# Modulation weights through four 1 MB buffers, and the first norm's statistics inside the prologue

## The reference

```python
m_lat = jnp.split((silu(c) @ ada_w[i] + ada_b[i])[:, None, :], 6, axis=-1)   # ada_w: (2, 1024, 6144)
m_ctx = jnp.split(silu(c_ctx) @ ada_w[i] + ada_b[i], 6, axis=-1)
h = rmsnorm(x, norm1_g[i]) * (1 + m[1]) + m[0]          # shift m[0], scale m[1]
x = x + m[2] * mixer(h)                                 # gate m[2]
x = x + m[5] * swiglu(rmsnorm(x, norm2_g[i]) * (1 + m[4]) + m[3])
filt = sin-MLP over positions (33 -> 64 -> 64 -> 2*512), times a window; then its Fourier transform
```

## Time and profile before

| | us |
|---|---|
| median of three runs | 3553.22 (3545.87 to 3558.02) |
| the profiled execution, its own time | 3556.72 |
| its span | 3555.1 |
| TensorE matmul busy | 3253.5 (92%) |
| VectorE busy | 1560.7 (44%) |
| ScalarE busy | 952.2 (27%) |
| GpSimd busy | 357.5 (10%) |
| modulation loads | 32 of 1536 KB, 7.7 from issue to landing (median) |

### The profile page before, as it was taken

How to read it: one execution, slowest core, us unless ns; L and a number is a source line. 1 busy time by engine, 2 the same in 40 slices (tenths; PEclk the granted TensorE clock), 3 DMA queues, 4 the chain that set the end, 5 groups by cost and what they waited for, 6 DMA issues and landing times. The chain is left out here.

```text
span 3555.1 us, 37659 instructions
## 1 busy us (share of the span) xinstructions
PE 3253.5 (92%) x15050; PEld 2512.4 (71%) x15050; DVE 1560.7 (44%) x1826; ACT 952.2 (27%) x1085; POOL 357.5 (10%) x252
## 2 busy tenths in 40 slices
PE   5878998799965799999999999899987899999999
PEld 2337885455554678888888888777766788888887
DVE  5305315666678533333223322567665432342333
ACT  2124112344411213111111111376773311111111
POOL 3000000077721110000000000200001000000000
PEclk8878999799987999999999999899998999999999
DMA  6772210000211411111111111201102111111112
GB/s 244 276 276 88 85 50 3 0 1 1 115 56 42 154 35 30 36 37 40 39 36 36 42 37 36 80 30 38 35 30 104 51 53 48 47 47 47 47 47 77
DMA packets 45560, 228.95 MB, mean 64 GB/s; under 512 B 6376, under 2 KB 6760, under 8 KB 39178
## 3 DMA queue, kind: packets, MB, share of 16 engines
q1 hardware_dynamic: 41594, 203.37, 16.6%
q10 hardware_dynamic: 1728, 13.63, 0.9%
q0 software_dynamic: 2128, 10.36, 0.7%
HBM read 201.65 MB, written 25.69 MB: 64 GB/s over the span
## 5 line engine op out<-in xcount | busy, mean ns | idle before, releaser
L252 PE MATMUL bank<-h_hi,w_hi 128*128 128x512 f32 (+1 forms) x2616 | 704.5, 369 | 15.3 <-DVE h_lo L1645 7.2
L252 PE MATMUL bank<-h_lo,w_hi 128*128 128x512 f32 (+1 forms) x2616 | 701.3, 368 | 0.0
L252 PE MATMUL bank<-h_hi,w_lo 128*128 128x512 f32 (+1 forms) x2616 | 700.7, 368 | 0.0
L238 DVE TENSOR_TENSOR w_lo<-w_raw,w_hi 128x1024 fp32r<-128x1024 f32 x194 | 262.6, 1354 | 662.8 <-ACT w_hi L232 658.0
L252 PEld LDWEIGHTS bank<-h_hi,w_hi 128*128 128x128 f32 x2616 | 452.9, 188 | 100.4 <-issue 15.7
L252 PEld LDWEIGHTS bank<-h_lo,w_hi 128*128 128x128 f32 x2616 | 453.0, 188 | 88.4 <-issue 3.1
L252 PEld LDWEIGHTS bank<-h_hi,w_lo 128*128 128x128 f32 x2616 | 452.7, 188 | 85.3
L1577 DVE SCALAR_TENSOR_TENSOR x<-bank,c_mods,x 128x1024 f32<-128x1024 f32 (+3 forms) x280 | 271.8, 1006 | 254.9 <-PE bank L252 254.8
L232 ACT ACTIVATE w_hi<-w_raw 128x1024 fp32r<-128x1024 f32 x194 | 203.8, 1051 | 647.2 <-PE bank L252 610.5
L252 PE MATMUL bank<-hid_hi,w_hi 128*128 128x512 f32 (+1 forms) x880 | 242.3, 373 | 11.6 <-DVE x L1577 11.6
L252 PE MATMUL bank<-hid_lo,w_hi 128*128 128x512 f32 (+1 forms) x880 | 240.1, 370 | 0.0
(11 more groups left out here) (284 smaller groups left out, 3673.3 us busy)
## 6 DMA issues: line engine op xcount, KB each, us to landing
w_raw<-in_weights SPq DMA_DIRECT2D x194, 512.0 KB, 3.5
ada_w<-in_ada_w SPq DMA_DIRECT2D x32, 1536.0 KB, 7.7
x<-in_x SPq DMA_DIRECT2D x2, 5120.0 KB, 18.6
h_gate<-u_scratch SPq DMA_DIRECT2D x4, 2560.0 KB, 9.3
u_scratch<-uc POOLq DMA_DIRECT2D x12, 640.0 KB, 3.2
spec_lat<-f_spec ACTq DMA_DIRECT2D x2, 3584.0 KB, 10.3
h_spec<-spec_lat SPq DMA_DIRECT2D x2, 3584.0 KB, 12.5
x_kept<-x SPq DMA_DIRECT2D x1, 4096.0 KB, 13.0
```

The source lines that it names most:

```text
L238: e.tensor_tensor(k.w_lo[s][:, :], k.w[s][:, :], k.w_hi[s][:, :].bitcast(F32), ALU.subtract).then_inc(k.split_lo[s], 1)
L252: mm = e.matmul(out[:, c:c + m], w[:, c1:c1 + P], x[:, c:c + m], start=(first and kk == 0 and n == 0), stop=(last and kk == kt - 1 and n = ...
```

## The change

- A modulation load holds two output tiles (`ADA_M = 2`, 1 MB), and there are 48, through four buffers. The SP issues them in an unrolled list; the one that reuses a buffer waits for the products four loads before. All loads share the semaphores for products, rows and columns.
- TensorE makes the products of load n and then turns the row of load n - 1. Products of load n wait until load n - 2 is stored. ScalarE copies row n, then stores the columns of load n - 1.
- 12 loads (`ADA_AT`) go in each product block, 1 behind each of the latent residues 2 to 6, and 14 are left for the end.
- In the order of loads the transform table goes ahead of x, and the modulation loads wait for the first hidden layer's matmuls. The clearing of `ss` waits for those of the second. `w12`, `w3` and the norm's `rr` are placed elsewhere.
- After the context transform of order 0 TensorE makes the first norm's sums and broadcasts in the prologue; the filter tiles of order 1 wait for the last copy to `rr`. VectorE scales and inverts behind its context butterfly, then makes the coefficients of norm 0 alone, which need the first eight loads. ScalarE takes root and copies to `rr` behind its store of the context spectrum.
- In `even_in` the norm begins with `xr = x * rr`. The other coefficients are made at the end of VectorE's list there (one bias addition for the first gate, one for the rest, and twelve small operations).

```diff
@@ class Norm
-        self.rr = k.at(f"rr{n}", R0 + T, [P, T])
+        self.rr = k.at(f"rr{n}", R0 + T if n else R0 + 5504, [P, T])
...
     def vector(self, k, e):
+        self.invert(k, e)
+        self.apply(k, e)
...
     def scalar(self, k, e):
+        self.root(k, e)
+        self.modulate(k, e)
@@ class Stream
-ADA_M = 3
+ADA_M = 2
 ADA_LOADS = 2 * 48 // ADA_M
+ADA_BUFS = 4
+ADA_FIRST = 2 * KT // ADA_M
...
     def load(self, k, e):
-        for s in range(2):
-            e.dma_start(self.w[s][:, :, :], k.d["ada_w"][s]).then_inc(self.full[s], 16)
-        with e.Fori(0, ADA_LOADS // 2 - 1) as i:
-            for s in range(2):
-                e.wait_ge(self.sums[s], i + 1)
-                e.dma_start(self.w[s][:, :, :], k.d["ada_w"][i * 2 + (s + 2)]).then_inc(self.full[s], 16)
+        for n in range(ADA_LOADS):
+            if n >= ADA_BUFS:
+                e.wait_ge(self.sums, n - ADA_BUFS + 1)
+            e.dma_start(self.w[n % ADA_BUFS][:, :, :], k.d["ada_w"][n]).then_inc(self.full[n % ADA_BUFS], 16)
+
+    def turn(self, k, e, n):
+        s = n % 2
+        e.wait_ge(self.read, n + 1)
+        for m in range(ADA_M):
+            tr = e.matmul(self.turned[s][:, 2 * m:2 * m + 2], self.row[s][:, m * P:(m + 1) * P],
+                          k.c["pick"][:, :], start=True, stop=True)
+        tr.then_inc(self.columns, 1)
 
     def products(self, k, e, count):
-        with e.Fori(0, count) as n:
...
+        for n in range(self.made, self.made + count):
+            s, w = n % 2, self.w[n % ADA_BUFS]
+            e.wait_ge(self.full[n % ADA_BUFS], 16 * (n // ADA_BUFS) + 16)
+            if n >= 2:
+                e.wait_ge(self.stored, n - 1)
+            for half in range(2):
+                for j in range(4):
+                    kk = 4 * half + j
+                    mm = e.matmul(self.group[s][j], k.silu_c[:, 32 * kk:32 * kk + 32], w[:, kk, :],
+                                  start=(half == 0), stop=(half == 1))
+            mm.then_inc(self.sums, 1)
+            if n:
+                self.turn(k, e, n - 1)
...
     def copy(self, k, e, count):
-        with e.Fori(0, count) as n:
...
+        for n in range(self.copied, self.copied + count):
+            s = n % 2
+            e.wait_ge(self.sums, n + 1)
+            if n >= 2:
+                e.wait_ge(self.columns, n - 1)
+            e.activation(self.row[s][:, :], self.out[s], ACT.Copy).then_inc(self.read, 1)
+            if n:
+                self.store(k, e, n - 1)
@@ prologue
+            e.dma_start(tab[:, :], d["tab_f"]).then_inc(tab_landed, 16)
             e.dma_start(k.x[:, :, :], d["x"]).then_inc(x_landed, 16)
-            e.dma_start(tab[:, :], d["tab_f"]).then_inc(tab_landed, 16)
...
+            e.wait_ge(mm_full, 1)
             ada.load(k, e)
...
+                    if g == NT:
+                        e.wait_ge(k.rr_ready, len(norm.chunks))
...
-                ada.products(k, e, 4)
+                ada.products(k, e, ADA_AT[order])
...
-                        if part == "lat" and pos in (2, 4):
+                        if part == "lat" and pos >= 2:
                             ada.products(k, e, 1)
-            ada.products(k, e, ADA_LOADS // 2 - ada.made)
+                if order == 0:
+                    e.wait_ge(hw_ready, NT)
+                    norm.tensor(k, e)
+            ada.products(k, e, ADA_LOADS - ada.made)
+            ada.turn(k, e, ADA_LOADS - 1)
...
-            ada.coefficients(k, e, steps)
+                if order == 0:
+                    norm.invert(k, e)
+                    e.wait_ge(others, 16 * len(names))
+                    e.wait_ge(ada.stored, ADA_FIRST)
+                    ada.coefficients(k, e, steps, [0])
...
                 e.dma_start(d["spec_" + part][order], spec[:, 0:2 * npos[part], :]).then_inc(stored, 16)
+                if j == 1:
+                    norm.root(k, e)
...
             e.memset(k.silu_c[:, :], 0.0).then_inc(padded, 1)
-            for s in range(2):
-                e.sem_inc(ada.stored[s], 1)
+            e.wait_ge(mm_full, 2)
             e.memset(k.ss[:, :], 0.0).then_inc(cleared, 1)
@@ even_in
-            norm.tensor(k, e)
             first_pair(k, e, w0, a0, k.rhs_h, (T, T), k.h_ready, norm.h_base)
...
-            norm.scalar(k, e)
+            norm.modulate(k, e)
...
-            norm.vector(k, e)
+            norm.apply(k, e)
...
             fold_gains(k, e)
+            k.ada.gate_bias(k, e, coef_steps)
+            k.ada.coefficients(k, e, coef_steps, [1, 2, 3])
```

More of the change, by code:

```diff
@@ L340, in scalar, with root @@
     def scalar(self, k, e):
+        self.root(k, e)
+        self.modulate(k, e)
+    def root(self, k, e):
         t, n = self.tiles, self.n
@@ L372, in __init__ @@
         words = KT * ADA_M * P
[L373 to L379, removed]
+        places = (S0, S0 + words, END - 2 * words, END - words)
+        assert 2 * words <= 4 * WS and H0 + 29056 <= END - 2 * words
+        self.w = [k.at(f"ada_w{n}", at, [P, KT, ADA_M * P]) for n, at in enumerate(places)]
+        self.full = [k.sem(f"ada_landed{n}") for n in range(ADA_BUFS)]
+        self.sums, self.read, self.stored, self.columns = (k.sem(f"ada_{n}") for n in ("sums", "read", "stored", "columns"))
         self.row = [k.at(f"ada_row{s}", H0 + 28544 + s * ADA_M * P, [P, ADA_M * P]) for s in range(2)]
@@ L386, in load @@
     def load(self, k, e):
-        for s in range(2):
-            e.dma_start(self.w[s][:, :, :], k.d["ada_w"][s]).then_inc(self.full[s], 16)
-        with e.Fori(0, ADA_LOADS // 2 - 1) as i:
-            for s in range(2):
-                e.wait_ge(self.sums[s], i + 1)
-                e.dma_start(self.w[s][:, :, :], k.d["ada_w"][i * 2 + (s + 2)]).then_inc(self.full[s], 16)
-    def products(self, k, e, count):
-        with e.Fori(0, count) as n:
-            i = n + self.made
-            for s in range(2):
[L399 to L412, removed]
@@ L413, in products, with store @@
         self.made += count
+    def store(self, k, e, n):
+        s = n % 2
+        e.wait_ge(self.columns, n + 1)
+        e.activation(k.mods[:, 2 * ADA_M * n:2 * ADA_M * (n + 1)], self.turned[s], ACT.Copy).then_inc(self.stored, 1)
     def copy(self, k, e, count):
-        with e.Fori(0, count) as n:
[L418 to L421, removed]
-            for s in range(2):
-                e.wait_ge(self.columns[s], i + 1)
-                e.activation(k.mods[:, bass.ds(i * (4 * ADA_M) + 2 * ADA_M * s, 2 * ADA_M)], self.turned[s], ACT.Copy
-                             ).then_inc(self.stored[s], 1)
+        for n in range(self.copied, self.copied + count):
+            s = n % 2
+            e.wait_ge(self.sums, n + 1)
[4 more added lines that the diff above has]
+                self.store(k, e, n - 1)
@@ L426, in copy, with coefficients @@
         self.copied += count
-    def coefficients(self, k, e, steps):
-        for s in range(2):
-            e.wait_ge(self.stored[s], ADA_LOADS // 2 + 1)
+    def coefficients(self, k, e, steps, norms):
+        first, last = 24 * norms[0], 24 * norms[-1] + (16 if len(norms) == 1 else 24)
         mods = k.mods[:, :].rearrange("p (m w) -> p m w", w=2)
-        bias = k.ada_b[:, :].unsqueeze(2).to_broadcast([P, 96, 2])
-        steps(e.tensor_tensor(mods, mods, bias, ALU.add))
-        for n in range(4):
+        part = mods[:, first:last, :]
+        bias = k.ada_b[:, first:last].unsqueeze(2).to_broadcast([P, last - first, 2])
+        steps(e.tensor_tensor(part, part, bias, ALU.add))
+        for n in norms:
@@ L442, in coefficients, with gate_bias @@
                 steps(e.tensor_copy(b, shift))
+    def gate_bias(self, k, e, steps):
+        mods = k.mods[:, :].rearrange("p (m w) -> p m w", w=2)[:, 16:24, :]
+        bias = k.ada_b[:, 16:24].unsqueeze(2).to_broadcast([P, 8, 2])
+        steps(e.tensor_tensor(mods, mods, bias, ALU.add))
 def butterfly_lat(e, steps, x, y, t):
@@ L706, in _ @@
                 if part == "lat":
-                    ada.copy(k, e, 4)
+                    ada.copy(k, e, ADA_AT[order])
                 if j:
@@ L718, in _ @@
                 e.dma_start(d["spec_" + part][order], spec[:, 0:2 * npos[part], :]).then_inc(stored, 16)
-            ada.copy(k, e, ADA_LOADS // 2 - ada.copied)
+                if j == 1:
+                    norm.root(k, e)
+            ada.copy(k, e, ADA_LOADS - ada.copied)
+            ada.store(k, e, ADA_LOADS - 1)
             e.wait_ge(stored, 64)
```

20 lines of the change are left out of this document (12 added, 8 removed).

## The result

| | before | after |
|---|---|---|
| median of five runs, us | 3553.22 (3545.87 to 3558.02) | 3572.93 (3569.28 to 3575.03) |
| profiled execution, its own time | 3556.72 | 3569.28 |
| its span | 3555.1 | 3567.6 |
| TensorE matmul busy | 3253.5 | 3275.0 |

The change makes the kernel slower by 19.7 us: the ratio of the times is 1.0053, with its 95% interval from 1.0040 to 1.0066. The forecast was 3549, and the range ended at 3567, 5.9 us short.

The account below looks back on a forecast made before the run. The prologue was taken as one chain on TensorE, whose products and DMA take turns. Its stages summed to xr at 273.8 instead of 278.1, net -4.3 us, so 3553.2 - 4.3 = 3549 us; range 3533 to 3567.

Parts of the forecast that it names:

- wait ahead of the tail: Before the last 14 loads: TensorE waits for ScalarE's store, context copies, root's table and row copy, 16.8 us.
- the one on the tiles: Filter tiles of order 1: they run at the high clock behind the norm's broadcasts, 9.6 us instead of 17.43.
- the 30 us for the second block: Second product block: twelve loads, between 26.6 us (fast) and 36.2 (slow), taken as 30.
- rival A: Tiles of order 1 and second block: low clock after TensorE's idleness, +14 us, 3563 in all; chance 0.27.
- the load beside the store: Spectrum stores: a modulation load sharing the DMA adds 0 to 2.4 us, taken as 2, and 1 at the tail.
- Rival C: Both spectrum stores share the engines with up to four loads, up to +14 us more, 3563; chance 0.05.
- The chain through ScalarE: Norm in the prologue: store, its wait, context copies, next store, table and root precede the broadcasts; 23.0 us with these.
- The hand-over: Product stream: one bare wait per load from the turn's end through the column store to the next products, 0.34 us.
- the cycle: Product stream, per 1 MB load: products, turn and hand-over, 3.15 us at 1.2 GHz, 1.77 at 2.4.
- A forward block starts slow: Forward blocks: the clock begins low and becomes fast, 1 to 4 us for the slow start.
- Rival B: Product blocks and tail: products keep 2.4 GHz and the DMA paces all, net -20 us, 3533; chance 0.15.
- Rival D: Norm's move: free, as ScalarE's wait overlaps nothing new, sum -18 us, 3535; chance 0.05.

Follow-up runs that it names:

- f1: The kernel after with twelve unused matmuls between the norm's sums and broadcasts and one more behind the broadcasts: 3559.55 us, 1.0009 of before.
- e7: The kernel after with the five woven loads behind residues 1 to 5 instead of 2 to 6: 3562.99 us, 1.0020 of before.
- e2: The kernel before with only the norm's move into the prologue, its loads and two buffers as before: 3573.27 us, 1.0045 of before.
- e1: The kernel after with the first norm put back to the start of the input projection, four buffers kept: 3551.35 us, 0.9985 of before.
- e4: The kernel after with the norm behind the context transform of order 1 and its root behind the latent store: 3545.50 us, 0.9972 of before.
- e3: The kernel after with twelve unused matmuls of 128 by 512 ahead of the norm's sums: 3566.64 us, 1.0029 of before.
- h1: g5 joined with e6's earlier copies and e7's weaving of the loads: 3533.94 us, 0.9930 of before.
- e6: e4 with ScalarE copying two loads' rows before it waits for the latent store of order 1: 3536.64 us, 0.9947 of before.
- g5: e4 with the turned columns in two banks of their own, so products need not wait for the column store: 3533.04 us, 0.9934 of before.

## Why the prediction was wrong

Its sum can be laid beside the trace, stage by stage. The difference at xr is 296.7 - 273.8 = 22.9 us. All rows are us; the first is a point in time, the others are lengths.

| stage | forecast | measured | |
|---|---|---|---|
| first products at | 59.0 | 58.66 | -0.3 |
| first block | 30 | 31.8 | +1.8 |
| to the last latent transform | 29.6 | 29.8 | +0.2 |
| norm in the prologue | 23.0 | 25.5 | +2.5 |
| tiles of order 1 | 9.6 | 17.3 | +7.7 |
| second block | 30 | 38.3 | +8.3 |
| to the last latent transform | 29.6 | 29.0 | -0.6 |
| wait ahead of the tail | 16.8 | 20.0 | +3.2 |
| tail | 42.1 | 42.7 | +0.6 |
| block's change and splits | 4.1 | 3.7 | -0.4 |

**The step that failed** is the one on the tiles: "The broadcasts raised the clock where they stand now; I take 9.6", and with it the 30 us for the second block. They make 16.0 of the 22.9 us. The row that it rested on, 1.00 at 277, follows broadcasts ahead of which TensorE had stood only 0.75 us, behind 4.40 us of sums; in the prologue it stood for 10.64 us, they ran slowly through, and the clock stayed at 0.50 through tiles and block. The evidence lay in the text as rival A, with its price (+14) and its test (a tile's spacing, 0.96 or 1.74 us; the first tile now takes 2.04 us at L644, and all ten 17.40). It was given 0.27 and should have been the forecast: the same prediction had already counted some 6 us of idleness for this place, and said of the tail, after a wait like it, "TensorE has idled, so the low clock". A's own 3563 would still have been 10 us short, for the reasons that follow. f1 shows the mechanism by filling the idleness and leaving the chain as it was.

**The second miss** is a size, the load beside the store: "0 to 2.4 us, I take 2", and 1 at the tail. It measured 4.4 and 5.2 us (e7), and the two waits in full, 14.33 and 15.15 us, are 5.7 more than the 11.95 (9.95 + 2) and 11.8 (10.8 + 1) taken. The upper bound assumed that a load delays the store by its own time alone. Rival C had the right place with the wrong count: one load is issued just ahead of the first store (121.37), and a second went out only in the course of the store of order 1 (238.88), whose excess is the larger. Not four loads.

**What held.** The chain through ScalarE (store, copies, store, table, root) came in its order; without the store's excess of 2.4 over the 11.95 taken for it, the norm's stretch is right to 0.1 us. The hand-over is 0.35 us for 0.34, the cycle 3.24 for 3.15. The stretches to the last latent transforms came out within 0.6 us, although "A forward block starts slow" isn't what the earlier trace rows show of the first one (1.00 throughout). The end of the prologue was near the forecast, 3.7 us from the last store to xr for 4.1, and the fourteen small operations at the end of the input projection took their place in VectorE's idleness: in front of the instruction of the earlier trace rows it is 30.49 us in the kernel after, for 33.36. With e7 worth 9.9 us and f1 13.4, the kernel after would stand 3.6 us below before, if the two add up, and the forecast was 4.3 below. No run has both, each of the two is uncertain by some 5 us, and the clock may have a share in e7's, so that sum is only argued.

**Rival B** (the products keep 2.4 GHz) came true in part, in the first loads of a block: in the kernel after the products of 62.72 to 69.03 took 1.07 us, and at 71.56 1.94, behind two waits for the DMA of 0.78 and 0.92 us. **Rival D**, the free move, is ruled out by e2.

At the end of the input projection the profiled executions are 17.6 us apart (572.12 for 554.57), and over the whole 12.6, while the medians are 19.7 apart. The kernel before was profiled in an execution 3.5 us above its median, the kernel after in one 3.6 below, and these make up the 7.1. What stays open is where, in the unchanged code behind 572, the 5 us from 17.6 to 12.6 lie.

## What to carry to other kernels

Before moving a step into an earlier block, write down for each engine that it crosses what it stands behind in program order; here a 0.2 us root had to stand out a store wait of 14 us. The same step, which in this place lost 17.7 us (e2), gained 5.9 over e1 when it was put into a gap of the same engine (e4). Price TensorE's idleness at its own length plus what the following stage loses at the low clock, which was larger here (13.4 us of time, f1, for 10.64 of idleness), and take the slow case as the forecast when the prediction itself counts several idle microseconds ahead of the stage. Put no load just ahead of a store that something waits for, and when a faster stream brings less than its cycle says, look at which in-order engine starts it.

## What the runs showed of the hardware

- A 1 MB load issued 0.5 us ahead of a 3.67 MB store on another queue makes the wait for the store 4.4 us longer, and 5.2 where a second load follows 7 us later; at 428 GB/s such a load would take 2.44 us, an estimate. Part of the excess lies at the start: from 121.4 to 124.0 the engines' share is 0.68 to 0.69 in the kernel after, but they move only 89 to 109 GB/s, and 299 to 467 from 124 to 130. Why they do is open.
- The filter tiles never raised a low clock: 17.40 us in e2, e7 and the kernel after, busy without a gap. A high one they kept (9.68 us in f1), but for e3, where it fell inside them. The twenty broadcasts ran at the low clock from idle (4.63 us). Behind the one-column sums and a gap of 0.75 us they took 2.56 us in e3 and e4, 4.13 in h1 and 4.64 in e6, so there the same order of work got either clock.
- The granted clock of a window is not always the clock of the work in it. In g5 the windows view shows 1.00 over a stretch

```profile
64.00:70.00 6.00, 6.00 (x45) 3.25 (x49) 6.00 (x11) 1.28 (x5) 0.00 (x0) 1.00 0.97 365
```

in which its timeline has the products at the low clock's 1.93 us:

```profile
64.03 1.93 PE L424 MATMUL bank<-ada_w,c_silu_c 128*32 128x256 f32 x16
...
66.84 1.93 PE L424 MATMUL bank<-ada_w,c_silu_c 128*32 128x256 f32 x16
```

  The duration of a known shape is the safer reading; the clocks told above were read from both.
